# Seven block products in place of eight for the input projections of a feed-forward and two MLPs

## The reference

```python
def swiglu(h, w_in, w_out):                    # hidden width 2816
    a, b = jnp.split(h @ w_in, 2, axis=-1)
    return (jax.nn.silu(a) * b) @ w_out
# second block, both layers; hidden width 4096
f = jnp.square(jax.nn.relu(h @ mlp_w1[i])) @ mlp_w2[i]
e = jax.nn.sigmoid(h @ ple_w_gate[i]) * (p[i] @ ple_w_proj[i])
x = layer_norm(DN_ALPHA * h + f + e, ln2_g[i], ln2_b[i])
```

## Time and profile before

| | us |
|---|---|
| median of three runs (2661.4 to 2662.5) | 2661.99 |
| span of the profiled execution, first to last instruction | 2657.4 |
| TensorE busy | 2605.5 |
| VectorE busy | 1202.9 |
| ScalarE busy | 972.6 |
| GpSimd busy | 962.0 |

### The profile page before, as it was taken

The page is one execution under the profiler, slowest core; times in us unless marked ns, Lnnn a source line. Parts: engine busy times, 40 slices in busy tenths (PEclk is TensorE's granted clock), DMA queues, the critical chain, the costliest instruction groups (busy, mean ns, idle before and its releaser), DMA issues.

```text
span 2657.4 us, 36222 instructions
## 1 busy us (share of the span) xinstructions
PE 2605.5 (98%) x14140; PEld 2104.0 (79%) x14140; DVE 1202.9 (45%) x2014; ACT 972.6 (37%) x1405; POOL 962.0 (36%) x257
## 2 busy tenths in 40 slices
PE   8999999999999999999999999999999999999998
PEld 6887788887777777888877688888877778888887
DVE  4575543343534344101248853715425665361542
ACT  4454521222533343222243843212235774221222
POOL 2312243434332223444433734444442113444442
PEclk9999999999999999999999999999999999999999
DMA  8623243543222212223222022222221111322221
GB/s 325 232 97 117 85 162 141 192 178 102 80 75 84 72 64 67 96 93 108 75 100 80 17 88 95 95 96 97 104 86 57 60 41 64 111 95 95 95 95 64
DMA packets 44032, 270.93 MB, mean 102 GB/s; under 512 B 4943, under 2 KB 8679, under 8 KB 15752
## 3 DMA queue, kind: packets, MB, share of 16 engines
q1 hardware_dynamic: 39888, 265.71, 28.2%
q10 hardware_dynamic: 4024, 3.54, 0.6%
HBM read 267.09 MB, written 2.13 MB: 101 GB/s over the span
## 4 chain that ended last, share of the span: by engine, by line
PE 70%; issue 22%; POOL 5%; DVE 2%; ACT 1%; POOLq 0%; ACTq 0%; DVEq 0%
PE lin L774 21%; PE lin L776 20%; PE lin L775 20%; POOL wlo L691 5%; PE lin L1326 2%; PE bank L1310 1%; PE bank L1344 1%; PE bank L1505 1%; PE bank L923 0%; PE lin L1330 0%; PE bank L1497 0%; PE lin L1497 0%; PE bank L1740 0%; PE bank L898 0%; DVE lr L3444 0%
## 5 line engine op out<-in xcount | busy, mean ns | idle before, releaser
L691 POOL TENSOR_TENSOR wlo<-raw,whi 128x2048 fp32r<-128x2048 f32 (+3 forms) x212 | 918.5, 4333 | 1650.6 <-ACT whi L1918 1650.6
L774 PE MATMUL lin<-hhi,whi 128*128 128x512 f32 x1960 | 776.5, 396 | 7.0 <-issue 2.6
L776 PE MATMUL lin<-hhi,wlo 128*128 128x512 f32 x1960 | 764.3, 390 | 0.0
L775 PE MATMUL lin<-hlo,whi 128*128 128x512 f32 x1960 | 763.9, 390 | 0.0
L1918 ACT ACTIVATE whi<-raw 128x2048 fp32r<-128x2048 f32 (+3 forms) x212 | 383.2, 1808 | 925.0 <-PE lin L776 863.8
L774 PE MATMUL lin<-ghi,whi 128*128 128x512 f32 x1136 | 446.5, 393 | 2.7 <-POOL wlo L691 2.0
L774 PEld LDWEIGHTS lin<-hhi,whi 128*128 128x128 f32 x1960 | 368.3, 188 | 99.3 <-issue 15.2
L776 PE MATMUL lin<-ghi,wlo 128*128 128x512 f32 x1136 | 442.8, 390 | 0.0
L775 PE MATMUL lin<-glo,whi 128*128 128x512 f32 x1136 | 442.6, 390 | 0.0
L776 PEld LDWEIGHTS lin<-hhi,wlo 128*128 128x128 f32 x1960 | 368.3, 188 | 78.4
L775 PEld LDWEIGHTS lin<-hlo,whi 128*128 128x128 f32 x1960 | 368.6, 188 | 74.6 <-issue 1.4
(11 more groups left out here) (487 smaller groups left out, 2728.5 us busy)
## 6 DMA issues: line engine op xcount, KB each, us to landing
raw<-in_w SPq DMA_DIRECT2D x171, 1024.0 KB, 4.9
adw_a<-in_ada SPq DMA_DIRECT2D x30, 1024.0 KB, 5.0
adw_b<-in_ada SPq DMA_DIRECT2D x18, 1024.0 KB, 5.8
raw<-in_w SPq DMA_DIRECT2D x20, 768.0 KB, 4.2
raw<-in_w SPq DMA_DIRECT2D x16, 640.0 KB, 3.8
raw<-in_w SPq DMA_DIRECT2D x5, 512.0 KB, 3.4
x<-in_x SPq DMA_DIRECT2D x1, 2048.0 KB, 9.8
out<-x SPq DMA_DIRECT2D x8, 256.0 KB, 2.1
```

The lines of the kernel that those rows point to most:

```text
L691: nc.gpsimd.tensor_tensor(wlo[:, slot, 0:size], raw[:, slot, 0:size], whi[:, slot, 0:size].bitcast(F32), ALU.subtract).then_inc(s.wlo_ok, 1)
L774: pe.matmul(dst, lh, rh, start=first, stop=False)
L775: pe.matmul(dst, lh, rl, start=False, stop=False)
L776: return pe.matmul(dst, ll, rh, start=False, stop=last)
```

## The change

`w` of a unit is seen as four blocks of four chunks by 128 columns, W00 W01 (chunks 0 to 3) and W10 W11 (chunks 4 to 7), and `h` as four quarters of four chunks by 256 tokens. Both output tiles, each in two halves of 256 tokens, come from seven block products instead of eight: each product is 4 chunks x 3 matmuls of 256 tokens. For that

- VectorE forms three sums of weight blocks into banks 4, 5 and 7 (`seven_sums`) and GpSimd one difference (`dif_ok`, in place, in `raw`); the seven blocks are split one by one: high parts on ScalarE (`block_high`), low parts of blocks 1, 2, 5 on VectorE (`block_low`) and of 0, 3, 4, 6 on GpSimd (`seven_lows`). All blocks of the next unit are made while TensorE is at this one, each once its product of this unit is done.
- Four sums of quarters of `h` are formed and split once a stage (`combined_sums`, `combined_high`, `combined_low`) in the upper halves of `ghi` and `glo`; so a part has at most eight hidden chunks: `FF_SHORT = (8, 8, 6)`, `FF2_PARTS = (8, 8, 8, 8)`.
- The seven products share four banks A, Q, U, V. Product 0 goes to A, 1 to Q, 2 onto U, 3 onto A, 4 onto U, 5 onto V, 6 onto U. U is seeded with A behind product 0, V with U behind product 2 (both ScalarE), and Q gets U plus product 1 behind product 4 and V gets product 1 added behind product 5 (both VectorE).
- The loops over unit pairs of these stages are written out.

18 of the 22 input units of the second feed-forward and the 16 of each MLP are changed. The first feed-forward isn't.

```diff
-FF2_PARTS = (16, 16)
+FF_SHORT = (8, 8, 6)
+FF2_PARTS = (8, 8, 8, 8)
...
 # SyncE, before it loads unit u
                 sp.wait_ge(s.wlo_ok, n.up(s.wlo_ok))
+                if u - 2 in ORDINAL:
+                    sp.wait_ge(s.sum_ok, HAD["sum_ok"] + 3 * ORDINAL[u - 2] + 3)
...
 # GpSimd, a unit (low_block waits for blk_hi of its block)
+                low_block(0, 0, 0, s.blk_lo_p)
+                pool.wait_ge(s.sum_ok, HAD["sum_ok"] + 3 * g + 1)
+                nc.gpsimd.tensor_tensor(weight_block(u, 0, 1), weight_block(u, 0, 0), weight_block(u, 0, 1),
+                                        ALU.subtract).then_inc(s.dif_ok, 1)
+                low_block(3, 1, 0, s.blk_lo_p)
+                low_block(4, 0, 1, s.blk_lo_p)
+                low_block(6, 1, 1, s.wlo_ok)
...
 # TensorE, a unit
+                    pe.wait_ge(s.blk_lo_p, HAD["blk_lo_p"] + 3 * g + 1)
+                    if u == u0:
+                        pe.wait_ge(st.ev, n.at(st.ev) + 2)
+                    else:
+                        pe.wait_ge(s.a_free, HAD["a_free"] + g)
+                    product(0, A, quarter(0, half0), True)
...
+                        pe.wait_ge(s.q_free, HAD["q_free"] + g)
+                    product(1, Q, combined(0), True)
...
+                    pe.wait_ge(s.seed_ok, HAD["seed_ok"] + 2 * g + 1)
+                    product(2, U, combined(1))
...
+                    product(3, A, quarter(4, half0))
...
+                    pe.wait_ge(s.seed_ok, HAD["seed_ok"] + 2 * g + 2)
+                    product(4, U, combined(2))
...
+                    product(5, V, quarter(4, half1))
...
+                    pe.wait_ge(s.c22_ok, HAD["c22_ok"] + g + 1)
+                    product(6, U, combined(3))
...
 # ScalarE, a unit (ahead(k): high part of the next unit's block k)
+                    act.wait_ge(s.prod_mm, HAD["prod_mm"] + 7 * g + 1)
...
+                    act.activation(U[:, half0], A[:, half0], ACT.Copy).then_inc(s.seed_ok, 1)
+                    if u > u0:
+                        hidden_high(u - 1, per - 1)
+                    ahead(0)
+                    act.wait_ge(s.prod_mm, HAD["prod_mm"] + 7 * g + 2)
+                    act.activation(p5, Q[:, half0], ACT.Copy).then_inc(s.p5_ok, 1)
+                    ahead(1)
+                    act.wait_ge(s.prod_mm, HAD["prod_mm"] + 7 * g + 3)
+                    if u > u0:
+                        act.wait_ge(s.y_ok, y0 + chunk0 + per * (u - u0))
+                    act.activation(V[:, half0], U[:, half0], ACT.Copy).then_inc(s.seed_ok, 1)
+                    ahead(2)
...
 # block_high: block 1 waits for the second sum, block 2 for the third
+                if k in (1, 2):
+                    act.wait_ge(s.sum_ok, HAD["sum_ok"] + 3 * g + k + 1)
+                elif k == 4:
+                    act.wait_ge(s.dif_ok, HAD["dif_ok"] + g + 1)
...
 # VectorE
+            def seven_sums(u):
...
+                v.tensor_tensor(as_block(B4), weight_block(u, 0, 1), weight_block(u, 1, 1), ALU.add).then_inc(s.sum_ok, 1)
+                v.wait_ge(s.sum_ok, HAD["sum_ok"] + 3 * g + 1)
+                v.tensor_tensor(as_block(B5), as_block(B4), weight_block(u, 0, 0), ALU.subtract).then_inc(s.sum_ok, 1)
+                v.wait_ge(s.sum_ok, HAD["sum_ok"] + 3 * g + 2)
+                v.tensor_tensor(as_block(B7), weight_block(u, 1, 0), as_block(B5), ALU.subtract).then_inc(s.sum_ok, 1)
...
 # VectorE, a unit (ahead(k): low part of the next unit's block k)
+                    if more:
+                        seven_sums(u + 1)
+                    ahead(1, 2)
...
+                    v.tensor_tensor(Q[:, half0], U[:, half0], p5, ALU.add).then_inc(s.c22_ok, 1)
...
+                    v.tensor_tensor(V[:, half0], V[:, half0], p5, ALU.add).then_inc(s.c12_ok, 1)
...
+                        times(V[:, half0], U, tmp[:, 0, half0], s.u_free)
+                        v.wait_ge(s.c22_ok, HAD["c22_ok"] + g + 1)
+                        times(V[:, half1], Q, tmp[:, 0, half1], s.q_free)
+                        ahead(5)
+                        hidden_low(V, 0, 1)
...
 # VectorE, start of the feed-forward (single(j): product and split of the hidden chunks of units 2 and 3)
+                chain(v.tensor_tensor(m[:, :, :], hhi[:, :, :].bitcast(F32), hlo[:, :, :].bitcast(F32), ALU.add))
+                combined_sums(0, m)
+                seven_sums(u)
+                single(0)
+                combined_low(0, 0)
+                combined_low(0, 1)
+                block_low(u, 1)
+                block_low(u, 2)
+                single(1)
+                combined_low(0, 2)
+                combined_low(0, 3)
+                block_low(u, 5)
```

More of the change, by code:

```diff
@@ L117, in stop_units @@
         if first:
-            while u < len(PLAN) and PLAN[u][0] in (last, "ffn_in", "mlp_in"):
+            while u < len(PLAN) and PLAN[u][0] in (last, "ffn_in", "mlp_in", "ffn_seven", "mlp_seven"):
                 u += 1
@@ L668, in _ @@
                 load(adw_c[k][:, :], ada_unit(46 + k), ada_in[k])
-            plain_units(44, len(plan))
+            for u in range(44, len(plan)):
+                next_unit(u, plan[u][1] * plan[u][2])
             for c in range(DC):
@@ L703, in lows, with seven_lows, low_block, all_lows @@
                         low(u % 2, size)
+            def seven_lows(u):
+                g = ORDINAL[u]
+                def low_block(k, rows, cols, done):
+                    pool.wait_ge(s.blk_hi, HAD["blk_hi"] + 7 * g + k + 1)
+                    b = block_at(u, k)
+                    nc.gpsimd.tensor_tensor(block_of_four(wlo, b), weight_block(u, rows, cols), block_of_four(whi, b).bitcast(F32),
+                                            ALU.subtract).then_inc(done, 1)
+                low_block(0, 0, 0, s.blk_lo_p)
[5 more added lines that the diff above has]
+                low_block(6, 1, 1, s.wlo_ok)
+            def all_lows(first, last):
+                u = first
+                while u < last:
+                    if u in ORDINAL:
+                        seven_lows(u)
+                        u += 1
+                        continue
+                    v = u
+                    while v < last and v not in ORDINAL:
+                        v += 1
+                    lows(u, v)
+                    u = v
             def gated_inputs():
@@ L1853, in mlp @@
+            def mlp(i, ends):
                 switch(s.ev_d)
                 lin_loop(4, hin, s.h_ok)
[L1855 to L1860, removed]
+                turned_y["mlp", i] = n.at(s.y_ok)
+                for part in range(4):
+                    seven_run(4, 1 + i if part == 0 else None)
+                    if part < 3:
+                        lin(8, hidden, s.y_ok)
@@ new lines, in out_run @@
+            def out_run(evict, follows=True):
+                for k in range(DC):
+                    act.wait_ge(s.mm, n.up(s.mm))
+                    if k < DC - 2:
+                        split_next()
+                    else:
+                        st.u += 1
+                    if evict is not None:
+                        evict(k)
+                    for j in {DC - 2: (0, 1, 2, 3), DC - 1: (4, 5, 6)}.get(k, ()):
+                        block_high(st.u + (DC - 1 - k), j)
+                tile[0] += DC
@@ L3554, in mlp @@
                             n.up(s.ev_d)
-                        tile[0] += 8
+                        else:
+                            out_sums(k)
+                        next_run(u, k)
+                    tile[0] += DC if part < 3 else 0
                 add_tiles(False)
```

401 lines of the change are left out of this document (345 added, 56 removed).

## The result

The changed kernel takes 2665.38 us (median of 13 runs, 2659.73 to 2670.47) against 2661.40 us (median of 13, 2658.23 to 2664.15) on the same chip: ratio 1.0017, 95% interval 1.0009 to 1.0024. It is 4 us slower; the forecast was 2670 us and +7.5. The prediction took 0.2%, 5.3 us, as the least that a measurement of this kernel can tell; by that bound the result is no change.

The account below looks back on a forecast made before the run. The prediction took TensorE's own pace to bound the kernel; -40.0 + 30.5 + 3.1 + 12.2 + 1.7 = +7.5 us on the median 2661.99 gave 2669.5, forecast 2670. Its own range was 2660 to 2680, with rivals 2634 to 2690.

Parts of the forecast that it names:

- A product of 12 matmuls costs 1.44 us, a unit 10.08: TensorE's new input units: 84 matmuls at 0.120 us each, saving 0.80 us a unit, 40.0 us over 50 units.
- Rival (d): TensorE: 256-column matmuls take half of 512, saving the full eighth, 68 us: 2642 us; chance with the rest 0.04.
- The ring: Inner units: product 4 waits for ScalarE's seed, queued behind VectorE's sums and block 1's high copy: 28 x 1.09 = 30.5 us.
- The walk: Hand-offs and durations followed from one product 4 to the next: 11.19 us with GpSimd first, 10.10 with VectorE first.
- GpSimd first by 0.04: Inner units: GpSimd's low part of block 0 starts at 7.45, VectorE's first sum at 7.49 and is held, ending at 9.27.
- Rival (a): Inner units: VectorE's sum gets in before GpSimd, or isn't held with output in PSUM: 2636 us; chance 0.27.
- Starts of runs: First units after output tiles: product 4 comes 0.66 us late in three runs, 0.16 in seven: 3.1 us.
- The feed-forward's first run: Second feed-forward: VectorE's work on combined inputs delays product 1 by 7.8 us, product 4 by 4.4 more: 12.2 us.
- 1.7 for the clock: Feed-forward's first run: TensorE's two idle times lower the clock to 0.50, costing 1.7 us (bounds 0 and 3.2).
- 1043.05: Time in us at which the first products of the feed-forward's first run would start in the kernel before.
- Output tiles, halves of weights, gates: nothing: Extra VectorE accumulations, bytes loaded in halves, output weights' splits and MLP gates' combined sums lie under cover: 0 us.
- The sum, +7.5: All terms together: 7.5 us slower on the profiled execution's 2657.4 us span, added to the median 2661.99: 2669.5 us.

Follow-up runs that it names:

- experiment 1: Changed kernel with GpSimd's low part of block 0 made to wait until VectorE's first sum is done: 2631.37 us, ratio 0.9895 to the kernel before.
- experiment 2: Changed kernel with a tiny useless GpSimd memset (0.10 us) ahead of block 0's low part in each unit: 2635.67 us, ratio 0.9906 to the kernel before.
- 3: Changed kernel with ScalarE's seed of bank V put ahead of the high copy of the next unit's block 1: 2633.92 us, ratio 0.9898.
- 6: Changed kernel with eight instead of four old-form units in the second feed-forward's first part, combined inputs made between them: 2654.59 us, ratio 0.9976.
- 8: Changed kernel with low part behind first sum, seed ahead of block 1's high copy, and eight old-form units in the feed-forward's first part: 2622.66 us, ratio 0.9863.
- the run with the lows held in 7: Changed kernel; in the feed-forward's first seven-product unit GpSimd's difference and last three low parts wait for VectorE's first two combined low parts: 2669.57 us, ratio 1.0029.
- experiment 4: An extra VectorE copy of 256 elements a row ahead of inner units' first sum: 2669.98 us on the changed kernel, 2642.85 with the low part behind that sum.
- without the rebuilding: Changed kernel with the rebuilding of h ahead of the feed-forward's combined inputs left out, so these come from stale values: 2665.36 us, ratio 1.0014.

## Why the prediction was right

The forecast was 2670 us, the median 2665.38; the mechanism, the place and nearly every size hold. By the prediction's own bound the outcome is no change, to which it gave 0.17, and not slower, to which it gave 0.54. By its own steps:

- **A product of 12 matmuls costs 1.44 us, a unit 10.08.** Measured 1.44 and 10.08. Rival (d), the full eighth, is out.
- **The ring, 28 units x 1.09 = 30.5.** The walk's 11.19 less 10.08 would have given 28 x 1.11 = 31.1; the 1.09 was taken against 10.10. Measured 28 inner units at 11.22 on average, 28 x 1.14 = 31.9; 25 are 11.18 or 11.19, as the walk had it. Experiments 1 to 3 show its two links, the order of the starts and the seed queued behind the second sum: undo either and it is gone.
- **GpSimd first by 0.04.** Measured 0.040 to 0.046. There was luck in it: both starts came 0.05 later than walked, which is more than the margin, and only because this error was common to both queues did the order stand. The open question was whether a sum with its output in PSUM is held like one that writes SBUF. It is: 1.80 us. Rival (a) failed on this margin and on nothing else, and experiment 2 shows that 0.1 us turns it; with the order turned the median was 2635.67, where (a) had said 2636. The rule of the Trainium skill ("SBUF — State Buffer", "Who interferes with whom"), which names no condition on the output and lets the first to start hold the port, agrees with the cases here: 28 sums that started 0.04 behind a low part were held (1.80 us), and six that were there when one low part ended and 0.02 ahead of the next were not (0.70 us). The held one ends 0.14 us sooner than its own length behind the other's end, whichever it is: the sum, 0.69 long, after 0.55, the low part, 1.29 long, after 1.15.
- **Starts of runs, 3.1.** 0.66 and 0.60 in each MLP's first two runs, nothing elsewhere: 2.5.
- **The feed-forward's first run, 12.2 and 1.7 for the clock.** Product 1 was forecast for 1052.3 and came at 1052.19. The unit took 21.84 us, 11.8 more than 10.08, and began 2.1 after 1043.05, of which 0.8 had arisen ahead of the stage: 13.1, against 13.9 forecast. The clock was underrated and this cancelled, by luck: it stood at 0.50 over product 1 and again from product 4 on, but product 4 had to wait for the seed anyway, so only products 4 to 6 paid, 5.88 - 4.32 = 1.6 us.
- **Output tiles, halves of weights, gates: nothing.** 43.55 us for eight tiles, no wait.
- **The sum, +7.5.** By these pieces -40.0 + 31.9 + 2.5 + 13.1 = +7.5, by the shifts between the traces +7.7.

What remains is the distance from +7.5 to the medians' +4.0 (2.4 to 6.4 by the interval). The shared stages explain how the profiled pair came to +11.3; why the typical run of the changed kernel is a few us under its sum was not settled. The half-clock stretches of the first run can't be it: a run that is spared them gains at most the 1.6 us paid there. The other versions show the same gap, in most cases. Read at the same instructions, their changed parts differ from before's by -27.1 us in experiment 1, -23.2 in 2, -26.2 in 3, -5.4 in 6 and -35.5 in 8, their medians by -30.1, -25.9, -27.5, -6.9 and -40.0; only the run with the lows held in 7 goes the other way (+7.6 and +8.0). So it seems that the stages both kernels share are 1 to 5 us shorter in these versions than in the median run of before; that is an inference, since the typical runs have no trace, and no run shows the reason. The step that is off is thus the last one, which carried the sum of a profiled execution over to the median as it stood.

## What to carry to other kernels

A saving on the bounding engine turns each helper engine's order of work into a chain with a deadline. Walk that ring once around with measured durations, write down every pair of starts on VectorE and GpSimd that lie within 0.1 us of each other, and settle their order by a wait instead of leaving it to the hand-offs: here 0.045 us decided 31 us in 2665. An error of the walk that is common to both starts does no harm; one of 0.05 us in a single queue would have turned this forecast. On an in-order engine put what the bound engine waits for (a seed) ahead of what is merely early (the next unit's copies): that alone cured the same ring with the collision still there. Where a new scheme needs inputs of its own, prepare them beside old-form work; the first run cost 13 us, and shortening its chain by 4.4 us returned 2.3 in the trace and nothing in the median.

## What the hardware did that I had not expected

- A held VectorE operation gets in at the boundary between two GpSimd operations that follow each other by 0.08 us, and it is then the second one that is stretched (1.29 to 1.61).
- A lead in the records can be negative and still win when GpSimd's operations follow each other: in experiment 2 VectorE's sum was recorded 0.01 us after GpSimd's low part, which followed another GpSimd operation, and kept its 0.69.
- One SBUF input can be enough. The copy into PSUM of experiment 4 started 0.05 us after a GpSimd operation and took its 0.42. The cast from SBUF to SBUF, without the rebuilding, started 0.09 us after one and took 1.49 where it takes 0.43 alone. The Trainium skill ("SBUF — State Buffer", "Who interferes with whom") counts casts among the operations that can take both port pairs. The prediction's walk of the first run had the cast as held, at 1.75 us; in the changed kernel it took 0.55 there. VectorE, then GpSimd in that kernel:

```profile
1038.62 1.49 DVE L3043 CAST ghi<-sq 128x512 fp32r<-128x512 f32 x1
...
1048.08 0.43 DVE L3043 CAST ghi<-sq 128x512 fp32r<-128x512 f32 x1
```

```profile
1038.53 1.29 POOL L775 TENSOR_TENSOR wlo<-raw,whi 128x512 fp32r<-128x512 f32 x1 [12.44 <-ACT whi L2422]
```

- The mean clock of one kernel's runs ranges over 0.003, and 0.003 of the span is 8 us, more than the difference between the two medians.
